# Two modulation stages and two norm stages at the head of a 1024-token kernel become one stage

## The chip, the cores and the metric

The kernel runs on one core of a Trainium2 chip. The metric is the device time of one execution in microseconds (us). A core has a matrix engine (TensorE, "PE" in the rows), a vector engine (VectorE, "DVE"), a scalar engine (ScalarE, "ACT"), GpSimd ("POOL") and SyncE ("SP"), which here issues nearly all of the DMA transfers. Each engine works through its own instructions in order; engines wait for one another by semaphores. SBUF is the on-chip memory with 128 partitions, PSUM the memory into which TensorE writes.

## The reference, cut to what matters

The model has two conditioned layers and then a second block of linear attention and experts. Only its head matters here. For each of the two layers a vector of 3 x 1024 modulation values is worked out for the latent tokens and another for the context tokens. The first layer's shift and scale are applied to the normed input:

```python
cond_l = jax.nn.silu(c)[:, None, :]
cond_c = jax.nn.silu(c_ctx)[None, None, :]
for layer in range(DEPTH):
    shift_l, scale_l, gate_l = jnp.split(cond_l @ w_ada[layer] + b_ada[layer], 3, axis=-1)
    shift_c, scale_c, gate_c = jnp.split(cond_c @ w_ada[layer] + b_ada[layer], 3, axis=-1)
    hl = rms_norm(x, norm_g[layer]) * (1.0 + scale_l) + shift_l
    hc = rms_norm(xc, norm_g[layer]) * (1.0 + scale_c) + shift_c
    ...
```

`w_ada` is (2, 1024, 3072) in float32, 12.6 MB for each layer; `x` has 1024 rows of 1024 features, `ctx` 256 rows. `hl` and `hc` are then multiplied by the layer's input weights `w_in0`.

## The kernel before

The program is a chain of stages. A `Stage` holds its SBUF and PSUM buffers and its semaphores, and inside it one block gives each engine its own instruction list; at a block's end all engines meet. So no instruction of a stage begins before the last of the stage before it has ended. The stages at the head, in order:

- `const` loads the identity matrix for transposes.
- `ada_0` and `ada_1` (`ada_stage`, lines 162 to 227) work out the modulation values of layer 0 and layer 1. The 3072 columns are cut into six chunks of 512. For each chunk, SP loads a weight piece `ada_w` of 2.1 MB (L190) and a bias piece (L192); TensorE multiplies with the two condition vectors as the stationary operand (L217), eight tiles of the inner dimension, each of which the trace shows as two records, so 16 a chunk; VectorE adds the bias (L227); SP stores two rows of 512 values to `ada` in DRAM (L196). There are two weight buffers, and the weights of chunk c + 2 are asked for when the matmuls of chunk c have ended.
- `n0l` (1024 latent rows) and `n0c` (256 context rows) are `norm_stage`, lines 230 to 378, two tiles of 128 rows a round. At its start SP loads gain, scale and shift, each spread over 128 partitions as 128 x 1024 (L269). For each tile: ScalarE squares and sums (L354), VectorE makes the mean (L316), GpSimd the power -0.5 (L366), VectorE multiplies by it and by the gain (L323) and adds the shift (L327), TensorE transposes in eight pieces of 128 x 128 (L378), and VectorE writes the result as a high part (L334) and a remainder (L337) into `h`, features by tokens.
- `in0` (`gemm_stage`) loads its first weight piece (L678), VectorE splits it in two (L718, L720), and TensorE begins (L706).

Semaphores are given out stage by stage and taken back by `recycle`, which clears them and lets all engines meet when more than a given number are out: 140 at the end of each stage. A later stage, `on0` (`out_norm`), already has the form of norm that the new stage uses: the rows are multiplied by the row's factor alone (L604), transposed (L483), and ScalarE applies scale and shift per feature as it takes them out of PSUM (L523), before VectorE splits them (L616, L618). It loads gain, scale and shift with features on partitions, as single elements of 4 bytes (L439).

Of the kernel before, what the change touches and what calls it, by code (L numbers as in the profile page):

```python
# [13 lines left out]
ACT = mybir.ActivationFunctionType  # L14
# [3 lines left out]
P = 128  # L18
D = 1024
KT = D // P  # L20
# [3 lines left out]
BANK = 512  # L24
EPS = 1e-6
# [4 lines left out]
F32R = mybir.dt.float32r  # L30
# [131 lines left out]
def ada_stage(nc, name, cond, w, b, out):  # L162

    N, cw = 3 * D, BANK
    rounds = N // (2 * cw)
    w_v = w.rearrange("(k p) n -> p k n", p=P)
    with Stage(nc, name) as st:
# [9 lines left out]
        with nc.Block() as block:  # L177

            @block.sync
            def _(sp):  # L180
                for j in range(2):
                    sp.dma_start(craw[:, j, :], cond[j].rearrange("(k p) -> p k", p=P), allow_slow_non_contiguous=True).then_inc(c_in, 16)
                for s in range(2):
                    w_in[s].open(sp)
                    o_out[s].open(sp)

                def load(it, s):
                    cols = ds((it * 2 + s) * cw, cw)
# [12 lines left out]

            @block.scalar
            def _(act):
                act.wait_ge(c_in, 32)
                for j in range(2):
                    act.activation(cond_t[:, :, j], craw[:, j, :], ACT.Silu).then_inc(c_ok, 1)

            @block.tensor
            def _(te):
                pe.open(te)  # L210
                te.wait_ge(c_ok, 2)
                with te.Fori(0, rounds) as it:
                    for s in range(2):
                        te.wait_ge(*w_in[s].now(it))
                        te.wait_ge(*dve.before(it, f"add{s}"))
                        for k in range(KT):
                            mm = te.matmul(ps[s][:], cond_t[:, k, :], wt[s][:, k, :], start=k == 0, stop=k == KT - 1)  # L217
                        mm.then_inc(*pe.did(f"mm{s}"))

            @block.vector  # L220
            def _(ve):
                dve.open(ve)
                with ve.Fori(0, rounds) as it:
                    for s in range(2):
                        ve.wait_ge(*pe.now(it, f"mm{s}"))
                        ve.wait_ge(*o_out[s].before(it))
                        ve.tensor_tensor(ot[s][:], ps[s][:], bt[s][:], ALU.add).then_inc(*dve.did(f"add{s}"))  # L227


def norm_stage(nc, name, ident, rows, x, norm_g, *, y=None, gate=None, scale=None, shift=None, x_out=None,  # L230
# [3684 lines left out]
def model(nc, x, c, ctx, c_ctx, norm_g, w_ada, b_ada, w_in0, sink0, gm_ln_g, gm_ln_b, gm_ws, gm_bs,  # L3915
# [10 lines left out]
    L = slice(0, S)  # L3926
# [5 lines left out]
    with ExitStack() as mem:  # L3932
        sb = lambda name, shape, dt=F32: mem.enter_context(nc.sbuf_tensor(name, shape, dt))
        ident_t, half_t = sb("ident", [P, P]), sb("half", [P, 1])
        with Stage(nc, "const") as st:
            loaded, ready = st.sem("loaded"), st.sem("ready")
            with nc.Block() as block:

                @block.sync
                def _(sp):  # L3940
                    sp.dma_start(ident_t[:], eye).then_inc(loaded, 16)
                    sp.wait_ge(loaded, 16)
# [19 lines left out]
        latent = ExitStack()  # L3962
# [124 lines left out]
```

## Time and profile before

| | us |
|---|---|
| median of 3 runs | 4587.3 |
| lowest and highest | 4581.42, 4588.21 |
| the profiled execution, its own time | 4582.68 |
| its span in the trace | 4580.8 |
| TensorE busy | 3749.5 |
| VectorE busy | 1923.9 |
| ScalarE busy | 1094.5 |
| GpSimd busy | 797.6 |

Busy shares are means over a program with many stages of different kinds. The mean granted TensorE clock of the span is 0.891 of full. In a row of a timeline the first number is the start in us from the span's start and the second the duration; "x32" joins 32 records in sequence; what stands in brackets is how long the engine had been idle and what ended that. "SPq" rows are DMA issues by SyncE: their duration is that of issuing, not of the transfer.

### The profile page before, as it was taken

Reading aid. Unit: us, or ns where it says so; the run is one execution under the profiler, and the core shown is the slowest. Engines: PE = TensorE matmul, PEld = TensorE weight load, DVE = VectorE, ACT = ScalarE, POOL = GpSimd, SP = SyncE. Lnnn points to the kernel's source line nnn. Section 1 sums busy time; section 2 is a strip of 40 time slices with the busy share of each in tenths; the row PEclk is TensorE's granted clock in tenths of the full one; section 3 lists DMA queues with packets and bytes.
Section 4 is the critical chain, followed back from the end, with each engine's and each line's share of the span. In section 5 each row is a group of like instructions: output and inputs, shape, how many; then the busy total and the mean of one; then the engine's idle time right before and its main releaser. Section 6 shows DMA issues by size and latency. Waiting matters only on the chain. (4 is left out here: it accounts for less than half of the span.)

```text
span 4580.8 us, 61052 instructions
## 1 busy us (share of the span) xinstructions
PE 3749.5 (82%) x24272; PEld 2811.9 (61%) x24272; DVE 1923.9 (42%) x2972; ACT 1094.5 (24%) x1970; POOL 797.6 (17%) x703
## 2 busy tenths in 40 slices
PE   7399799478859999977999899885879996759991
PEld 1299644467634444446988788662479995746661
DVE  0511144542137888855223255404546667211113
ACT  0111123222023444441111122215223333111111
POOL 0000000000013444440000021202134441020002
PEclk9699789588969999988999999886989997779996
DMA  6322200331110000002311144221333436379975
GB/s 221 111 85 72 72 7 12 123 108 50 50 37 3 4 3 3 3 28 103 114 60 64 62 101 102 93 71 35 87 105 95 120 97 236 138 261 335 326 242 197
DMA packets 333288, 462.23 MB, mean 101 GB/s; under 512 B 88853, under 2 KB 238821, under 8 KB 331765
## 3 DMA queue, kind: packets, MB, share of 16 engines
q1 hardware_dynamic: 325482, 433.18, 29.5%
q0 software_dynamic: 7568, 25.70, 1.5%
q8 instruction: 170, 2.79, 0.3%
q14 instruction: 68, 0.56, 0.0%
HBM read 350.73 MB, written 107.99 MB: 100 GB/s over the span
## 5 line engine op out<-in xcount | busy, mean ns | idle before, releaser
L2130 PE MATMUL gp_ps_p<-gp_wh,m 128*128 128x512 f32 (+1 forms) x1408 | 410.0, 373 | 7.5 <-DVE gp_wl L2174 7.5
L706 PE MATMUL in_ps_p<-in_wh,h 128*128 128x352 f32 x1280 | 309.5, 325 | 15.0 <-DVE in_wl L720 15.0
L2130 PEld LDWEIGHTS gp_ps_p<-gp_wh,m 128*128 128x128 f32 x1408 | 260.8, 189 | 47.7 <-DVE gp_wl L2174 8.0
L2130 PE MATMUL gp_ps_p<-gp_wl,m 128*128 128x512 f32 (+1 forms) x704 | 262.1, 372 | 0.0
L3785 PE MATMUL ex_ps_g<-ex_wgu,ex_xt 128*128 128x256 f32 x1024 | 234.8, 389 | 27.1 <-ACT ex_xt L3819 13.3
L1960 DVE TENSOR_REDUCE lq_nc<-lq_ps_f 128x1 f32<-128x512 f32 (+1 forms) x384 | 215.0, 585 | 59.3 <-PE lq_ps_f L1814 56.5
L1915 ACT ACTIVATE lq_p<-lq_ps_s 128x512 f32<-128x512 f32 x320 | 191.1, 598 | 181.5 <-PE lq_ps_s L1836 172.6
L706 PEld LDWEIGHTS in_ps_p<-in_wh,h 128*128 128x128 f32 x1280 | 224.1, 190 | 15.3 <-issue 15.3
L3785 PEld LDWEIGHTS ex_ps_g<-ex_wgu,ex_xt 128*128 128x128 f32 x1024 | 196.2, 194 | 60.7 <-DVE ex_xt L3836 19.4
L474 PE MATMUL on_ps_a<-on_wh,m 128*128 128x512 f32 x576 | 188.2, 404 | 43.1 <-DVE on_wl L567 36.5
L2034 POOL TENSOR_TENSOR lq_acc<-lq_acc,lq_p 128x512 f32<-128x512 f32 x128 | 172.1, 1345 | 242.2 <-ACT lq_p L1915 241.7
L706 PE MATMUL in_ps_p<-in_wl,h 128*128 128x352 f32 x640 | 207.0, 323 | 0.0
L2297 PE MATMUL cg_ps_p<-m,cg_wh 128*128 128x512 f32 x768 | 183.3, 397 | 0.0
L1982 DVE TENSOR_TENSOR lq_acc<-lq_acc,lq_p 128x512 f32<-128x512 f32 x128 | 167.8, 1311 | 15.6 <-ACT lq_p L1915 13.8
L1814 PE MATMUL lq_ps_f<-lq_kh,lq_qh 96*128 96x512 f32 (+1 forms) x384 | 143.9, 404 | 25.2 <-DVE lq_nc L1960 15.9
L2297 PEld LDWEIGHTS cg_ps_p<-m,cg_wh 128*128 128x128 f32 x768 | 144.7, 191 | 29.5
L3078 PE MATMUL dr_ps_big<-dr_px,dr_pn 64*64 64x128 f32 (+1 forms) x3072 | 160.5, 245 | 0.3 <-issue 0.3
L1846 PE MATMUL lq_ps_o<-lq_p,lq_v 128*64 128x512 f32 x640 | 159.4, 620 | 0.0
L474 PEld LDWEIGHTS on_ps_a<-on_wh,m 128*128 128x128 f32 x576 | 112.6, 196 | 68.8 <-DVE on_wl L567 37.8
L1836 PE MATMUL lq_ps_s<-lq_qh,lq_kh 97*128 97x512 f32 x320 | 147.5, 461 | 0.0
L2130 PEld LDWEIGHTS gp_ps_p<-gp_wl,m 128*128 128x128 f32 x704 | 132.8, 189 | 20.0
L3078 PEld LDWEIGHTS dr_ps_big<-dr_px,dr_pn 64*64 64x64 f32 x3072 | 137.6, 135 | 3.3 <-issue 3.1
(551 smaller groups left out, 7372.8 us busy)
## 6 DMA issues: line engine op xcount, KB each, us to landing
ex_wgu<-in_moe_w_gate_dram SPq DMA_DIRECT2D x32, 1024.0 KB, 8.2
ex_wgu<-in_moe_w_up_dram SPq DMA_DIRECT2D x32, 1024.0 KB, 10.7
ex_wd<-in_moe_w_down_dram SPq DMA_DIRECT2D x32, 1024.0 KB
ada_w<-in_w_ada_dram SPq DMA_DIRECT2D x12, 2048.0 KB
gp_w<-in_w_in_dram SPq DMA_DIRECT2D x32, 512.0 KB, 4.3
dr_qk<-feat SPq DMA_DIRECT2D x32, 512.0 KB, 4.2
yb<-ex_y SPq DMA_DIRECT2D x32, 512.0 KB
p<-in_o SPq DMA_DIRECT2D x8, 1760.0 KB, 7.2
```

Source lines behind the costliest of these rows:

```text
L474: mm = te.matmul(acc[i % NA][:, b, :], a, c, start=k == 0 and p == 0, stop=k == KT - 1 and p == 2)
L706: mm = te.matmul(ps[n % NB][:, 0:cw], a, b, start=n_ == 0, stop=n_ == len(todo) - 1)
L1836: mm = te.matmul(ps[e][t % 2][:], k_[e][b][:, cols], q_[e][c][:], start=n == 0, stop=n == 2)
L1846: mm = te.matmul(po[e * VC:(e + 1) * VC, :], vt[:, kt, h * VC:(h + 1) * VC], pt[e][t % NBUF][:], start=kt == 0, stop=kt == nk - 1)
L1915: act.activation(pt[e][t % NBUF][:], ps[e][t % 2][:], ACT.Exp, scale=scale).then_inc(exp_s, 1)
L1960: ve.tensor_reduce(nc_[v % 2][:, i, c:c + 1], f[:, 0:hi - lo], AX.X, ALU.max, negate=True).then_inc(freed_s[n % RING], 1)
L1982: ve.tensor_tensor(a[:], pt[0][(t - 1) % NBUF][:] if kt == 1 else a[:], pt[0][t % NBUF][:], ALU.add).then_inc(add_a, 1)
L2034: gp.tensor_tensor(a[:], pt[1][(t - 1) % NBUF][:] if kt == 1 else a[:], pt[1][t % NBUF][:], ALU.add).then_inc(add_b, 1)
L2130: mm = te.matmul(ps[i][:, 0:width[c]], a, b, start=k == 0 and p == 0, stop=k == KT - 1 and p == 2)
L2297: mm = te.matmul(ps[u % 2][:, hf, :], a[:, k, :], h_t[:, h, k, cols].bitcast(F32R), start=part == 0 and n == 0, stop=part == 1 and n == le ...
L3078: mm = te.matmul(b4[rows, h, js], P_[rows, h, :], old[rows, h, js, :], start=True, stop=True)
L3785: mm = te.matmul(pg[s % 2][:, g * DE:(g + 1) * DE], x_t[s][:, k * P:(k + 1) * P], wgu[s][:, g, k, :], start=k == 0, stop=k == KT - 1)
```

## The change

A new function `ada_norm` takes the place of `ada_0`, `ada_1`, `n0l` and `n0c`. It is one stage. The twelve weight chunks of both layers run in one sequence through three weight buffers. All ten tiles of rows stay in SBUF (`an_x`); their loads stand in SP's list after chunks 0 to 3, three, three, three and one. Their squares, sums and row factors are worked out while the chunks run. After chunk 3 the scale and shift of layer 0 are complete in DRAM; SP waits for these stores and loads them with features on partitions. The transposes stand in TensorE's list in pairs of tiles after chunks 5, 6, 7, 8 and 9. ScalarE applies scale and shift, VectorE splits into `h`. A second `recycle` with the bound 80 stands before `latent_pairs`.

```diff
+def ada_norm(nc, ident, half, cond, w_ada, b_ada, ada, segs, g, h_t):
...
+    cw, WB, X = BANK, 3, range(2)
+    per = 3 * D // cw
+    NC_ = 2 * per
+    need = 2 * D // cw
...
+    turns = {need + 1 + j: [2 * j, 2 * j + 1] for j in range(n // 2)}
...
+            @block.sync
+            def _(sp):
+                def weights(c):
+                    s, b = divmod(c, per)
+                    if c >= WB:
+                        sp.wait_ge(mm_s, c - WB + 1)
+                    sp.dma_start(wt[c % WB][:], w_ada[s].rearrange("(k p) n -> p k n", p=P)[:, :, b * cw:(b + 1) * cw]).then_inc(w_in[c % WB], 16)
+                    if c >= 2:
+                        sp.wait_ge(add_s, c - 1)
+                    sp.dma_start(bt[c % 2][:], b_ada[s].rearrange("(a n) -> a n", a=1)[:, b * cw:(b + 1) * cw].to_broadcast([2, cw])).then_inc(b_in[c % 2], 16)
...
+                for c in range(WB - 1):
+                    weights(c)
+                sp.dma_start(g_t[:], g.rearrange("(k p) -> p k", p=P), allow_slow_non_contiguous=True).then_inc(g_in, 16)
+                at = 0
+                for c in range(NC_):
+                    if c + WB - 1 < NC_:
+                        weights(c + WB - 1)
+                    for i in range(at, min(at + 3, n)):
+                        sp.dma_start(xt[i][:], src[i]).then_inc(x_in[i], 16)
+                    at = min(at + 3, n)
+                    store(c)
+                    if c == need - 1:
+                        for b in X:
+                            sp.wait_ge(o_out[b], 16 * (need // 2))
+                        for k in range(len(segs)):
+                            for t, part in ((sc_t, 1), (sh_t, 0)):
+                                sp.dma_start(t[:, k, :], ada[0][k, part * D:(part + 1) * D].rearrange("(k p) -> p k", p=P),
+                                             allow_slow_non_contiguous=True).then_inc(p_in, 16)
...
+            @block.tensor
+            def _(te):
+                te.wait_ge(c_ok, 2)
+                for c in range(NC_):
+                    te.wait_ge(w_in[c % WB], 16 * (c // WB + 1))
+                    if c >= 2:
+                        te.wait_ge(add_s, c - 1)
+                    for k in range(KT):
+                        mm = te.matmul(ps[c % 2][:], cond_t[:, k, :], wt[c % WB][:, k, :], start=k == 0, stop=k == KT - 1)
+                    mm.then_inc(mm_s, 1)
+                    for i in turns.get(c, []):
+                        te.wait_ge(hn_s, i + 1)
+                        if i >= 2:
+                            te.wait_ge(af_s, i - 1)
+                        for k in range(KT):
+                            tr = te.transpose(tp[i % 2][:, k // 4, (k % 4) * P:(k % 4 + 1) * P], xt[i][:, k * P:(k + 1) * P], ident)
+                        tr.then_inc(tr_s, 1)
...
+                for i in range(n):
+                    act.wait_ge(tr_s, i + 1)
+                    if i >= 2:
+                        act.wait_ge(e1_s, i - 1)
+                    for k in range(KT):
+                        ins = act.activation(tmp[i % 2][:, k, :], tp[i % 2][:, k // 4, (k % 4) * P:(k % 4 + 1) * P], ACT.Identity,
+                                             bias=sh_t[:, seg_of[i], k:k + 1], scale=sc_t[:, seg_of[i], k:k + 1])
+                    ins.then_inc(af_s, 1)
...
+                done = 0
+                for c in range(NC_):
+                    bias(c)
+                    if c < need:
+                        top = min(done + 3, n)
+                        for i in range(done, top):
+                            scaled(i)
+                        for i in range(done, top):
+                            normed(i)
+                        done = top
+                    if c == need:
+                        ve.wait_ge(g_in, 16)
+                        ve.wait_ge(p_in, 32 * len(segs))
+                        for k in range(len(segs)):
+                            ve.scalar_tensor_tensor(sc_t[:, k, :], sc_t[:, k, :], 1.0, g_t[:], ALU.add, ALU.mult).then_inc(gg_s, 1)
+                    for i in turns.get(c - 1, []):
+                        leave(i)
...
-        for i in range(2):
-            ada_stage(nc, f"ada_{i}", [c[0], c_ctx], w_ada[i], b_ada[i], ada[i])
...
-            for nm, rows, src, r in (("n0l", L, x, 0), ("n0c", X, ctx, 1)):
-                norm_stage(nc, nm, ident, rows.stop - rows.start, src, norm_g[0], scale=part(ada[0], r, 1), shift=part(ada[0], r, 0),
-                           h_t=h[:, :, :, rows])
+            ada_norm(nc, ident, half, [c[0], c_ctx], w_ada, b_ada, ada, [(len(lat), x), (len(con), ctx)], norm_g[0], h[:, :, :, :])
...
+            recycle(nc, 80)
```

In `ada_norm`, `bias(c)` waits for the matmuls of chunk c and adds the bias; `scaled(i)` waits for the square of tile i; `normed(i)` waits for GpSimd's power and multiplies the tile; `leave(i)` waits for ScalarE and splits tile i into `h`.

SyncE's list in the kernel before, from the third weight piece of `ada_0` on (a loop of three rounds): `ada_w` is a weight piece, `ada_b` a bias piece, `ada<-ada_o` a store.

```order
L190 DMA ada_w<-in_w_ada_dram 128x8x512
L192 DMA ada_b<-in_b_ada_dram 2x512
L196 ISA
L196 DMA ada<-ada_o 2x512
L189 REGISTER_ALU
L190 ISA
```

The same place in the changed kernel, from the fifth weight piece to the seventh: `an_w` is a weight piece, `an_b` a bias piece, `an_x` a tile of rows, `an_sc` and `an_sh` the scale and shift per feature.

```order
L266 DMA an_w<-in_w_ada_dram 128x8x512
L269 DMA an_b<-in_b_ada_dram 2x512
L286 DMA an_x<-in_x_dram 128x1024 x2
L286 DMA an_x<-in_ctx_dram 128x1024
L274 DMA ada<-an_o 2x512
L266 DMA an_w<-in_w_ada_dram 128x8x512
L269 DMA an_b<-in_b_ada_dram 2x512
L286 DMA an_x<-in_ctx_dram 128x1024
L274 DMA ada<-an_o 2x512
L294 DMA an_sc<-ada 128x8x1
L294 DMA an_sh<-ada 128x8x1
```

The row loads and the four element-wise loads now stand between weight pieces; the pair of scale and shift is issued twice, and the seventh weight piece (chunk 6) follows it.

VectorE's list in the changed kernel, from the bias of chunk 0 to that of chunk 2 (`an_o` is a chunk's result, `an_ss` the row factors):

```order
L350 TENSOR_TENSOR an_o0<-an_ps_p0,an_b0 2x512
L354 TENSOR_SCALAR an_ss<-an_ss 128x1 x3
L358 TENSOR_SCALAR an_x0<-an_x0,an_ss 128x1024
L358 TENSOR_SCALAR an_x1<-an_x1,an_ss 128x1024
L358 TENSOR_SCALAR an_x2<-an_x2,an_ss 128x1024
L350 TENSOR_TENSOR an_o1<-an_ps_p1,an_b1 2x512
```

Before, two bias additions followed each other with nothing between them; now three tiles' row factors and products stand between them.

TensorE's list in the changed kernel, from chunk 5 to chunk 7 (`an_ps_t` receives the transposes):

```order
L307 MATMUL an_ps_p1<-an_w2,an_cond 2x512 x8
L314 MATMUL an_ps_t0<-ident,an_x0 128x128 x8
L314 MATMUL an_ps_t1<-ident,an_x1 128x128 x8
L307 MATMUL an_ps_p0<-an_w0,an_cond 2x512 x8
L314 MATMUL an_ps_t0<-ident,an_x2 128x128 x8
L314 MATMUL an_ps_t1<-ident,an_x3 128x128 x8
L307 MATMUL an_ps_p1<-an_w1,an_cond 2x512 x8
```

The transposes, which had stages of their own behind the last chunk, stand between chunks of the same sequence.

## Rows read from the trace of the kernel before

**Rows 1.** The head of the page: span and instruction count.

```profile
span 4580.8 us, 61052 instructions
```

**Rows 2.** Timeline of the head of the program, 0 to 201 us.

```profile
4.24 0.37 SPq L190 DMA_DIRECT2D ada_w<-in_w_ada_dram  x1
...
12.12 15.73 PE L217 MATMUL ada_ps_p<-ada_w,ada_cond 128*2 128x512 f32 x32 [12.12 <-DMA ada_b<-in_b_ada_dram]
...
21.11 0.68 DVE L227 TENSOR_TENSOR ada_o<-ada_ps_p,ada_b 2x512 f32<-2x512 f32 x1 [21.11 <-PE ada_ps_p L217]
21.18 0.40 SPq L190 DMA_DIRECT2D ada_w<-in_w_ada_dram  x1
...
29.14 13.90 PE L217 MATMUL ada_ps_p<-ada_w,ada_cond 128*2 128x512 f32 x32 [1.29 <-DMA ada_b<-in_b_ada_dram]
...
102.56 14.18 PE L217 MATMUL ada_ps_p<-ada_w,ada_cond 128*2 128x512 f32 x32 [1.12 <-DMA ada_b<-in_b_ada_dram]
...
119.16 0.38 SPq L269 DMA_DIRECT2D n0l_g<-in_norm_g_dram  x1
...
200.28 11.68 SPq L678 DMA_DIRECT2D in_w<-in_w_in_dram  x3
```

**Rows 3.** Groups of instructions, 0 to 211 us; busy us, mean ns, idle.

```profile
L217 PE MATMUL ada_ps_p<-ada_w,ada_cond 128*2 128x512 f32 x192 | 87.4, 612 | 29.4 <-DMA ada_b<-in_b_ada_dram 29.1
...
L354 ACT ACTIVATE n0l_sq<-n0l_x 128x1024 f32<-128x1024 f32 x8 | 8.5, 1057 | 88.8 <-DMA n0l_x<-in_x_dram 87.2 <-DVE h L334 1.6
```

**Rows 4.** Windows while one weight piece moves; last: clock, DMA share, GB/s.

```profile
24.00:25.00 1.00, 1.00 (x3) 0.17 (x2) 0.00 (x0) 0.00 (x0) 0.00 (x0) 1.00 1.03 399
...
28.00:29.00 1.00, 0.00 (x0) 0.00 (x0) 0.56 (x1) 0.00 (x0) 0.00 (x0) 1.00 0.16 53
```

**Rows 5.** Timeline of stage `on0`, the new norm's operations.

```profile
1020.32 2.88 ACT L523 ACTIVATE on_tmp<-on_ps_t,on_sh,on_sc 128x128 f32<-128x128 f32 x8
...
1023.24 0.69 DVE L616 CAST m<-on_tmp 128x1024 fp32r<-128x1024 f32 x1 [4.00 <-ACT on_tmp L523]
...
1023.97 1.23 DVE L618 TENSOR_TENSOR m<-on_tmp,m 128x1024 fp32r<-128x1024 f32 x1
...
1025.33 0.55 POOL L546 TENSOR_TENSOR on_ss<-on_ss,half 128x1 f32<-128x1 f32 x1 [14.24 <-DVE on_ss L583]
...
1025.92 0.75 DVE L604 TENSOR_SCALAR on_h<-on_x,on_ss 128x1024 f32<-128x1024 f32 x1 [0.66 <-POOL on_ss L546]
...
1028.33 1.03 PE L483 MATMUL on_ps_t<-ident,on_h 128*128 128x128 f32 x8
```

**Rows 6.** Timeline of stage `on0`, five element-wise loads by SyncE.

```profile
967.10 0.44 SPq L439 DMA_DIRECT2D on_g<-in_norm_g_dram  x1
...
971.83 0.58 SPq L439 DMA_DIRECT2D on_sh<-ada  x1
...
974.27 0.24 DVE L623 SCALAR_TENSOR_TENSOR on_sc<-on_sc,on_g 128x8 f32<-128x8 f32 x2 [1.56 <-DMA on_sh<-ada]
```

**Rows 7.** Windows around idle TensorE; third from the end: granted clock.

```profile
121.00:122.00 1.00, 0.00 (x0) 0.00 (x0) 0.00 (x0) 0.00 (x0) 0.00 (x0) 0.83 1.11 168
...
122.00:123.00 1.00, 0.00 (x0) 0.00 (x0) 0.00 (x0) 0.00 (x0) 0.00 (x0) 0.50 0.72 262
...
70.00:73.00 3.00, 2.69 (x4) 0.47 (x5) 0.00 (x0) 0.00 (x0) 0.00 (x0) 0.50 1.04 388
...
74.00:75.00 1.00, 1.00 (x3) 0.17 (x2) 0.00 (x0) 0.00 (x0) 0.00 (x0) 1.00 0.70 256
```

**Rows 8.** Timeline at two stage ends, with and without `recycle`.

```profile
1251.36 0.60 ACT L1640 ACTIVATE gate_t<-in1g_ps_p 128x512 f32<-128x512 f32 x1 [4.84 <-PE in1g_ps_p L1633]
...
1253.82 0.37 SPq L678 DMA_DIRECT2D in1c_w<-in_w_in_dram  x1
...
1317.39 0.59 ACT L1540 ACTIVATE kpe_t<-lp_ps_t 32x512 f32<-32x512 f32 x1 [0.49 <-PE lp_ps_t L1586]
...
1318.31 0.38 SPq L1754 DMA_DIRECT2D lq_p<-in_w_kvb_dram  x1
```

More of the change, by code:

```diff
@@ L227, in _, with store, bias, scaled @@
                         ve.tensor_tensor(ot[s][:], ps[s][:], bt[s][:], ALU.add).then_inc(*dve.did(f"add{s}"))
+def ada_norm(nc, ident, half, cond, w_ada, b_ada, ada, segs, g, h_t):
[3 more added lines that the diff above has]
+    need = 2 * D // cw
+    n = sum(seg[0] for seg in segs)
+    seg_of = [k for k, seg in enumerate(segs) for _ in range(seg[0])]
+    src = [seg[1][i * P:(i + 1) * P, :] for seg in segs for i in range(seg[0])]
+    turns = {need + 1 + j: [2 * j, 2 * j + 1] for j in range(n // 2)}
+    order = [i for c in sorted(turns) for i in turns[c]]
+    assert order == list(range(n)) and max(turns) < NC_
+    with Stage(nc, "an") as st:
+        craw, cond_t = st.sb("craw", [P, 2, KT]), st.sb("cond", [P, KT, 2])
+        wt = [st.sb(f"w{b}", [P, KT, cw]) for b in range(WB)]
+        bt, ot = ([st.sb(f"{t}{b}", [2, cw]) for b in X] for t in ("b", "o"))
+        xt = [st.sb(f"x{i}", [P, D]) for i in range(n)]
+        sq, ss = st.sb("sq", [P, D]), st.sb("ss", [P, n])
+        g_t, sc_t, sh_t = st.sb("g", [P, KT]), st.sb("sc", [P, 2, KT]), st.sb("sh", [P, 2, KT])
+        tmp = [st.sb(f"t{b}", [P, KT, P]) for b in X]
+        ps = [st.ps(f"p{b}", [2, cw]) for b in X]
+        tp = [st.ps(f"t{b}", [P, 2, BANK]) for b in X]
+        c_in, c_ok, g_in, p_in, gg_s = (st.sem(t) for t in ("c_in", "c_ok", "g_in", "p_in", "gain"))
+        w_in, b_in, o_out = ([st.sem(f"{t}{b}") for b in range(k)] for t, k in (("w_in", WB), ("b_in", 2), ("o_out", 2)))
+        x_in = [st.sem(f"x_in{i}") for i in range(n)]
+        mm_s, add_s, sq_s, va_s, rs_s, hn_s, tr_s, af_s, e0_s, e1_s = (st.sem(t) for t in (
+            "mm", "add", "square", "var", "rsqrt", "hn", "tr", "affine", "ev0", "ev1"))
+        with nc.Block() as block:
+            @block.sync
[8 more added lines that the diff above has]
+                    sp.dma_start(bt[c % 2][:], b_ada[s].rearrange("(a n) -> a n", a=1)[:, b * cw:(b + 1) * cw].to_broadcast([2, cw])).then_inc(b_in[c % 2], 16)
+                def store(c):
+                    s, b = divmod(c, per)
+                    sp.wait_ge(add_s, c + 1)
+                    sp.dma_start(ada[s][:, b * cw:(b + 1) * cw], ot[c % 2][:]).then_inc(o_out[c % 2], 16)
+                for j in X:
+                    sp.dma_start(craw[:, j, :], cond[j].rearrange("(k p) -> p k", p=P), allow_slow_non_contiguous=True).then_inc(c_in, 16)
+                for c in range(WB - 1):
[16 more added lines that the diff above has]
+                                             allow_slow_non_contiguous=True).then_inc(p_in, 16)
+                for b in X:
+                    sp.wait_ge(o_out[b], 16 * (NC_ // 2))
+            @block.tensor
[15 more added lines that the diff above has]
+                        tr.then_inc(tr_s, 1)
+            @block.scalar
+            def _(act):
+                act.wait_ge(c_in, 32)
+                for j in X:
+                    act.activation(cond_t[:, :, j], craw[:, j, :], ACT.Silu).then_inc(c_ok, 1)
+                for i in range(n):
+                    act.wait_ge(x_in[i], 16)
+                    if i:
+                        act.wait_ge(sq_s, i)
+                    act.activation(sq[:], xt[i][:], ACT.Square, accum_out=ss[:, i:i + 1]).then_inc(sq_s, 1)
+                act.wait_ge(gg_s, len(segs))
+                for i in range(n):
+                    act.wait_ge(tr_s, i + 1)
[5 more added lines that the diff above has]
+                    ins.then_inc(af_s, 1)
+            @block.gpsimd
+            def _(gp):
+                for i in range(n):
+                    gp.wait_ge(va_s, i + 1)
+                    gp.tensor_tensor(ss[:, i:i + 1], ss[:, i:i + 1], half, ALU.pow).then_inc(rs_s, 1)
+            @block.vector
+            def _(ve):
+                def bias(c):
+                    ve.wait_ge(mm_s, c + 1)
+                    ve.wait_ge(b_in[c % 2], 16 * (c // 2 + 1))
+                    if c >= 2:
+                        ve.wait_ge(o_out[c % 2], 16 * (c // 2))
+                    ve.tensor_tensor(ot[c % 2][:], ps[c % 2][:], bt[c % 2][:], ALU.add).then_inc(add_s, 1)
+                def scaled(i):
+                    ve.wait_ge(sq_s, i + 1)
+                    ve.tensor_scalar(ss[:, i:i + 1], ss[:, i:i + 1], 1.0 / D, EPS, ALU.mult, ALU.add).then_inc(va_s, 1)
+                def normed(i):
+                    ve.wait_ge(rs_s, i + 1)
+                    ve.tensor_scalar(xt[i][:], xt[i][:], ss[:, i:i + 1], None, ALU.mult).then_inc(hn_s, 1)
+                def leave(i):
+                    rows = slice(i * P, (i + 1) * P)
+                    ve.wait_ge(af_s, i + 1)
+                    ve.tensor_copy(h_t[:, 0, :, rows].bitcast(F32R), tmp[i % 2][:]).then_inc(e0_s, 1)
+                    ve.wait_ge(e0_s, i + 1)
+                    ve.tensor_tensor(h_t[:, 1, :, rows].bitcast(F32R), tmp[i % 2][:], h_t[:, 0, :, rows], ALU.subtract).then_inc(e1_s, 1)
+                done = 0
[15 more added lines that the diff above has]
+                        leave(i)
+                for i in turns.get(NC_ - 1, []):
+                    leave(i)
```

## The prediction

> **What bounds the kernel now.** I read the head of the page for the span [rows 1], then the timeline of the head of the program [rows 2], since the change touches nothing else but one `recycle`. Stages do not overlap, so what the head takes adds to the end in full: `in0` cannot ask for its first weight piece before 200.28 us. The whole question is by how much that issue moves.
>
> In [rows 2] the reader is to see three stretches. (a) `ada_0` asks for its first weights at 4.24 and TensorE starts at 12.12; the twelve chunks of both stages end at 102.56 + 14.18 = 116.74. Twelve at 6.9 (below) would be 83 of these 105 us; the rest is the second start, waits of 1.1 to 1.3 us before each pair, and the low clock after each start. (b) The norm stage's first issue stands at 119.16, 2.4 us after that last matmul: bias, store, landing, meeting. (c) From 119.16 to 200.28, 81.1 us, the two norm stages run. They hold ten tiles on a chain of VectorE, and TensorE hardly works.
>
> The grouped rows [rows 3] give the floor: 192 matmul records busy for 87.4 us in the ada stages, and only 29.4 us of idle before them. A pair of chunks takes 13.90 us without a disturbance [rows 2], so 6.9 us each; the first pair, which starts at the low speed, takes 15.73. VectorE's first bias stands at 21.11, so chunk 0 ends at about 21.1.
>
> **What the change does, step by step.** The unit is the time at which TensorE ends chunk c, E(c); E(0) = 21.1 stays, as the first issues are the same.
>
> Transfers. A weight piece asked for at 21.18 on an empty queue serves TensorE at 29.14 at the latest [rows 2]. While it moves the queue carries 399 GB/s, and by 28 to 29 us it is empty [rows 4]; I take 390 GB/s. So 2.1 MB take 5.4 us, with 1.5 us before and 1.0 behind. A tile of rows (0.52 MB) takes 1.35. I assume that the queue serves in the order of issue.
>
> Chunks 0 to 3 hold the row work. Bias 0 ends at 21.8. SP then issues a bias piece and three tiles (2.0 us until the first moves), the tiles move for 4.0, and the last lands 1.0 later. ScalarE's square is 1.06 [rows 3], with its accumulator read about 1.25. VectorE's mean and GpSimd's power take 0.2 and 0.55, three products 0.75 each [rows 5], the next bias 0.68 [rows 2]. The sum is 11.5 with the gaps between them, so biases 1, 2 and 3 end at 33.3, 44.8 and 56.3, where TensorE's own pace would be 6.9. What is queued behind: VectorE can't add bias c + 1 while it waits for the rows of round c, and SP holds back the next bias piece, and with it the rows and the next weights, until that bias is added. The third buffer carries chunks 1 to 3 (E(1) = 27.9, E(2) = 34.8, E(3) = 41.7). Weights 4, behind three tiles, land at 45.8: TensorE waits 4.1. Weights 5 land at 57.3 where E(4) = 52.7: it waits 4.6. E(5) = 64.2.
>
> Parameters. After bias 3 (56.3) the tenth tile and the store move, behind weights 5; the store has landed at about 61. Then SP issues the four element-wise loads. Their price is shown by the same form in `on0`: five such loads take from 967.10 to 974.27, 7.2 us, of which SP issues until 972.4 [rows 6]. I take 1.3 us of SP for each, 5.2 together (bounds: 0.6 each, as the last one's 0.58, and 2.0). VectorE has its parameters near 68.6 and delays only bias 5. But weights 6 are asked for behind these loads, at 66.3, and land at 66.3 + 1.5 + 5.4 + 1.0 = 74.2. TensorE ends chunk 5 and its pair of transposes at 64.2 + 2.1 = 66.3 (1.03 us for eight [rows 5]) and waits 7.9. That is the dearest wait of the new stage.
>
> From chunk 6 on the transfers are ahead (weights 7 and 8 land near 79.6 and 85.0), and TensorE sets the pace: 6.9 + 2.1 = 9.0 us for chunks 6 to 9, 6.9 for 10 and 11. Beside it, a pair of tiles costs ScalarE 2 x 2.88 and VectorE 2 x (0.69 + 1.23) [rows 5]. Their chain over the two buffers is bias 0.7, one split 2.0, two outputs 5.8: 8.5 us a round. It hides under 9.0, but by half a microsecond only. So E(11) = 74.2 + 4 x 9.0 + 2 x 6.9 = 124.0.
>
> Clock. Idle TensorE loses its full clock some 5 us after its last matmul: it ended at 116.74 and the granted clock is 0.83 in the row of 121 to 122 and 0.50 in the next. After the restart at 70.3 it stays at 0.50 (1.2 GHz) until about 74, then 1.00 (2.4 GHz) [rows 7]. The waits of 4.1 and 4.6 are at the edge; what they would cost is hidden by the next wait for weights. The wait of 7.9 is past it and nothing hides the restart: 15.73 - 13.90 = 1.8 us [rows 2]. E(11) = 125.8.
>
> End. From the last matmul to the next stage's first issue 2.4 us, as now. `in0` asks for its weights at 128.2 instead of 200.28: 72 us less. What `in0` does from there is the same.
>
> `recycle`. With 10 semaphores fewer at the head, the clearing moves from behind `in1g` to behind `latent_prep`, and the new call with 80 finds none out. With it a stage end takes 1.9 us (ACT ends 1251.96, issue 1253.82), without it 0.3 (1317.98, 1318.31) [rows 8]: one is saved, one is paid, nothing is left.
>
> Removed without a separate term: gain, scale and shift spread over 128 partitions (six loads of 512 KB), VectorE's product with the gain and its addition of the shift, both inside the 81.1 us.
>
> **The rivals.**
> 1. Transfers hide everything: three buffers and early rows are enough. Then E(11) = 21.1 + 11 x 6.9 + 5 x 2.1 = 107.5 and the gain is 90 us: 4497. For it speaks that all bytes (30 MB at 390 GB/s, 78 us) fit under the matmuls. Against it, the chain of 11.5 us a round, which bandwidth doesn't shorten.
> 2. ScalarE and VectorE are the bound behind chunk 5, or SP's four loads take 2.0 each. The half microsecond of cover goes if an output takes a tenth longer: +4 to +8 us over four rounds; dearer loads add 3. Gain 60 to 68: 4519 to 4528.
> 3. The clock doesn't come back after the wait of 7.9. Six chunks at 13.7 and four pairs at 3.6 make E(11) = 171; the gain is 27: 4560. Were the whole stage at the low clock, 12.1 + 12 x 13.7 + 5 x 3.6 = 194.5 gives 197 against 200.28, no change that can be told. Against it: in both ada stages the clock is full within 4 us [rows 7], with TensorE as busy as here. The Trainium skill has the rule that speaks for this rival (TensorE: Matmul & The Clock Gate, section HAM oscillation): a kernel that waits for a transfer at each tile sees its clock fall at each of them, and with the three waits here in a row it would give the 4560 of this paragraph at worst.
> 4. Slower than before: the element-wise loads. They are 4096 pieces of 4 bytes on SP's only queue, and weights 6 stand behind them. They would have to take 72 us more than I count, 77 instead of 5. [rows 6] shows 5120 such pieces within 7.2 us; that would need over ten times the price, perhaps because they now share the queue with weights.
>
> The Trainium skill (DMA: Bandwidth & Descriptors, Specifications) states that line rate needs 512 B or more and that smaller pieces are read, changed and written back. The rule speaks for rival 4's direction; the trace has the price at the size in question.
>
> **How the numbers follow.** The schedule above: 0.60, gain 64 to 80. Rival 2: 0.15. Rival 1, whole or in good part: 0.15. Rival 3, whole or in part: 0.08, of which 0.02 without any measurable change. Rival 4: 0.02. The sum is made against the profiled execution, 4582.7 with its span of 4580.8 [rows 1]: 4510.7. The median of the runs shown is 4.6 us higher, so I predict 4587.3 - 72 = 4515. The range 4499 to 4531 takes in rival 2, the likeliest case and the partial form of rival 1. About 0.2%, 9 us, is what a measurement of this kernel can tell from no change. Faster by more: 0.96; within: 0.02; slower: 0.02.
>
> **What would show it.** In the trace after: `in_w` issued near 128 us; bias additions of the new stage some 11 us apart at chunks 1 to 3; three waits of TensorE for weights before chunks 4, 5 and 6, the last the longest; after it, starts of chunks 9 us apart and a granted clock of 1.00; no wait of TensorE for ScalarE. The prediction is wrong if rows land much earlier or later than 7 us after their issue begins, if weights overtake rows in the queue, or if VectorE's work on ten tiles reaches behind chunk 11.

## The result

The changed kernel takes 4501.6 us (median of four runs, 4489.9 to 4508.3) against 4587.3 of the kernel before (four runs, 4581.4 to 4588.2): ratio 0.9821, 95% interval 0.9806 to 0.9836. It is faster by 86 us; 72 had been forecast, with a range of 4499 to 4531. Three later comparisons stand under the experiments; two with this same kernel give 0.9802 (0.9780 to 0.9823) and 0.9804 (0.9785 to 0.9824), so the first one is the smallest of three.

The profiled execution is the fastest of its four, 4489.9 us. The head of its page has the span and TensorE's busy time, to be held against [rows 1]:

```profile
span 4488.1 us, 60788 instructions
...
PE 3727.8 (83%) x24272; PEld 2796.0 (62%) x24272; DVE 1900.9 (42%) x2962; ACT 1123.4 (25%) x2048; POOL 796.8 (18%) x701
```

The timeline of the head of the program answers to [rows 2]. `an_ps_p` rows of TensorE are weight chunks (x16 is one chunk), `an_ps_t` rows transposes:

```profile
12.45 29.11 PE L307 MATMUL an_ps_p<-an_w,an_cond 128*2 128x512 f32 x64 [12.45 <-DMA an_w<-in_w_ada_dram]
...
21.00 0.68 DVE L350 TENSOR_TENSOR an_o<-an_ps_p,an_b 2x512 f32<-2x512 f32 x1 [21.00 <-PE an_ps_p L307]
...
25.63 1.06 ACT L326 ACTIVATE an_sq<-an_x 128x1024 f32<-128x1024 f32 x1 [19.14 <-DMA an_x<-in_x_dram]
...
31.76 0.67 DVE L350 TENSOR_TENSOR an_o<-an_ps_p,an_b 2x512 f32<-2x512 f32 x1
...
42.38 0.67 DVE L350 TENSOR_TENSOR an_o<-an_ps_p,an_b 2x512 f32<-2x512 f32 x1
...
44.44 7.03 PE L307 MATMUL an_ps_p<-an_w,an_cond 128*2 128x512 f32 x16 [2.88 <-DMA an_w<-in_w_ada_dram]
...
53.26 0.67 DVE L350 TENSOR_TENSOR an_o<-an_ps_p,an_b 2x512 f32<-2x512 f32 x1
...
54.64 0.29 SPq L274 DMA_DIRECT2D ada<-an_o  x1
...
55.26 8.72 PE L307 MATMUL an_ps_p<-an_w,an_cond 128*2 128x512 f32 x16 [3.79 <-DMA an_w<-in_w_ada_dram]
...
57.72 0.38 SPq L294 DMA_DIRECT2D an_sc<-ada  x1
...
60.27 0.58 SPq L266 DMA_DIRECT2D an_w<-in_w_ada_dram  x1
...
68.34 7.03 PE L307 MATMUL an_ps_p<-an_w,an_cond 128*2 128x512 f32 x16 [2.46 <-DMA an_w<-in_w_ada_dram]
...
77.20 7.03 PE L307 MATMUL an_ps_p<-an_w,an_cond 128*2 128x512 f32 x16
```

The same timeline from chunk 8 to `in0`:

```profile
86.05 7.03 PE L307 MATMUL an_ps_p<-an_w,an_cond 128*2 128x512 f32 x16
...
103.77 13.89 PE L307 MATMUL an_ps_p<-an_w,an_cond 128*2 128x512 f32 x32
...
117.70 0.68 DVE L350 TENSOR_TENSOR an_o<-an_ps_p,an_b 2x512 f32<-2x512 f32 x1 [2.46 <-PE an_ps_p L307]
...
120.31 1.02 SPq L836 DMA_DIRECT2D in_w<-in_w_in_dram  x2
```

The reader is to see three things. First, chunks 0 to 3 run in one piece (29.11 us for 64 records, no wait in it), then TensorE waits 2.88, 3.79 and 2.46 us for the weights of chunks 4, 5 and 6, and never again. Second, VectorE's biases of chunks 1, 2 and 3 stand at 31.76, 42.38 and 53.26, a good 10.6 us apart, although the matmuls of these chunks were done by then (those of chunk 3 ended at 41.56); in the trace before the first two such rows stood at 21.11 and 27.88, 6.8 us apart. Third, from chunk 6 on a chunk begins every 8.86 us (77.20, 86.05). `in0` asks for its weights at 120.31 instead of 200.28: 80.0 us earlier, 7.9 more than forecast.

The groups for the same stretch, against [rows 3]: the matmuls cost what they cost before (86.9 us), their idle time is down from 29.4 to 21.6 us, of which 12.4 is the start, and the transposes are 9.8 us with no idle ahead of them.

```profile
L307 PE MATMUL an_ps_p<-an_w,an_cond 128*2 128x512 f32 x192 | 86.9, 610 | 21.6 <-DMA an_w<-in_w_ada_dram 21.6
...
L333 ACT ACTIVATE an_t<-an_ps_t,an_sh,an_sc 128x128 f32<-128x128 f32 x80 | 28.5, 496 | 22.6 <-DVE h L365 16.7 <-PE an_ps_t L314 5.9
...
L314 PE MATMUL an_ps_t<-ident,an_x 128*128 128x128 f32 x80 | 9.8, 276 | 0.0
```

The span is 92.7 us shorter, though, and 80.0 of that lie ahead of `in0`. The other 12.7 lie behind it, in stages whose instructions the change leaves as they are. The first experiments are about that.

### The profile page after: what moved, and what is told of

Read it like the earlier page. It is cut to its first block and busy times, and to the rows that moved or that the text cites. A ratio compares the mean times of both kernels' runs of the same rounds, so it can differ in the third digit from the quotient of the medians.

```text
span 4488.1 us, 60788 instructions
## 1 busy us (share of the span) xinstructions
PE 3727.8 (83%) x24272; PEld 2796.0 (62%) x24272; DVE 1900.9 (42%) x2962; ACT 1123.4 (25%) x2048; POOL 796.8 (18%) x701
## 6 DMA issues: line engine op xcount, KB each, us to landing
ex_wgu<-in_moe_w_up_dram SPq DMA_DIRECT2D x32, 1024.0 KB, 10.7
```

## The experiments

"The issue" is the start of `in0`'s first weight load in a run's own trace. It measures the new stage alone; whole times scatter by some 10 us each way.

**1. The changed kernel again, unaltered, and a third time.**

> The changed kernel once more, unaltered. In the first trace in0 asked for its weights at 120.31 us, 80.0 earlier than before, yet the span was 92.7 shorter. Theory A (the change acts at the head alone; the other 12.7 us are scatter between executions, four runs lay between 4490 and 4508): the issue stands again at 120.3 within half a us, and the time from there to the end of the span, 4367.8 in the first trace, comes out longer, nearer to the 4380.5 of before. Theory B (the stages behind became shorter through the moved clearing of semaphores or other addresses): the rest is again 4368 within 3 us.

> The changed kernel a third time. In two traces in0 asked at 120.3 and 125.0 us; the difference lay in the waits for weights 4 to 6 and in slow matmuls behind them. Theory (which of the waits is long enough to lose the clock is a matter of a few tenths of a us and of the execution): again between 119 and 126, with one or two chunks of more than 8 us among chunks 4 to 6. Rival (the second run's chip was slower): 120.3 again, one such chunk.

The issue stood at 124.95 in the second trace and at 122.54 in the third; the rest was 4375.9 and 4365.8. TensorE's chunks 4, 5 and 6 in the second trace:

```profile
45.85 8.33 PE L307 MATMUL an_ps_p<-an_w,an_cond 128*2 128x512 f32 x16 [3.14 <-DMA an_w<-in_w_ada_dram]
...
56.69 7.03 PE L307 MATMUL an_ps_p<-an_w,an_cond 128*2 128x512 f32 x16 [2.51 <-DMA an_w<-in_w_ada_dram]
...
70.20 9.81 PE L307 MATMUL an_ps_p<-an_w,an_cond 128*2 128x512 f32 x16 [4.58 <-DMA an_w<-in_w_ada_dram]
```

and in the third:

```profile
45.05 8.72 PE L307 MATMUL an_ps_p<-an_w,an_cond 128*2 128x512 f32 x16 [3.54 <-DMA an_w<-in_w_ada_dram]
...
55.77 8.72 PE L307 MATMUL an_ps_p<-an_w,an_cond 128*2 128x512 f32 x16 [2.00 <-DMA an_w<-in_w_ada_dram]
...
68.88 8.72 PE L307 MATMUL an_ps_p<-an_w,an_cond 128*2 128x512 f32 x16 [2.49 <-DMA an_w<-in_w_ada_dram]
```

A chunk takes 7.03 us at full clock and 8.3 to 9.8 where it restarts at the low one. The first trace has one such chunk, the second two, the third three, of one and the same program, behind waits of much the same length. With the length of the waits it makes the scatter of the head, 120.3 to 125.0 us. My expectation that the head repeats within half a us was wrong, and the rest of the second trace, 4375.9, fits neither of its two theories. For the third run the issue lay between 119 and 126 as expected, but with three slow chunks and not one or two. Whole times: 4495.8 (five runs) against 4584.6, and 4491.4 (four) against 4585.7.

**2. The chunks merged, the norm stages left.** `ada_norm` without its rows, then the old loop, and the second `recycle` as in the changed kernel:

```diff
-            ada_norm(nc, ident, half, [c[0], c_ctx], w_ada, b_ada, ada, ...)
+        ada_only(nc, [c[0], c_ctx], w_ada, b_ada, ada)   # sync, tensor and vector lists of ada_norm, without rows
...
+            for nm, rows, src, r in (("n0l", L, x, 0), ("n0c", X, ctx, 1)):
+                norm_stage(nc, nm, ident, ...)
```

> The twelve chunks in one stage with three weight buffers, but without rows; the two norm stages as before. Theory: this removes the second start of the chunks (12.0 us of idle TensorE), one slow restart (1.8) and four waits of 1.1 to 1.3 before pairs (5.1), 18.9 in all: in0 asks at 181.4 instead of 200.3. Rival (two buffers were not the cause of the waits before pairs): they stay, 14 us, in0 asks at 186.

The time was 4560.1, ratio 0.9948 (0.9931 to 0.9966). TensorE ran all 192 records without a wait:

```profile
12.36 85.19 PE L280 MATMUL an_ps_p<-an_w,an_cond 128*2 128x512 f32 x192 [12.36 <-DMA an_w<-in_w_ada_dram]
```

```profile
181.43 11.84 SPq L747 DMA_DIRECT2D in_w<-in_w_in_dram  x3
```

The issue stood at 181.4, what the theory said; that it fits to the tenth is luck, since the head scatters by more. With three buffers and no rows in the queue the chunks have no wait at all, so the waits in the new stage come with the rows and parameters.

**3. The new stage with all transposes behind chunk 11.**

```diff
-    turns = {need + 1 + j: [2 * j, 2 * j + 1] for j in range(n // 2)}
+    turns = {NC_ - 1: list(range(n))}
```

> The new stage, but all ten tiles are transposed behind chunk 11 and none between chunks. Theory: chunks end at 109 to 110 us, then ScalarE sets the pace with 2.9 us a tile: 29 us, one split 2, in0 asks at 142, 22 us behind the changed kernel. Rival (ScalarE and VectorE hand each tile over and don't overlap, 4.9 us a tile): in0 asks at 160.

4520.7 us, ratio 0.9860 (0.9845 to 0.9875), issue at 145.2. Behind the last chunk ScalarE works in one piece and the others follow it, a tile each 2.8 us:

```profile
114.64 28.02 ACT L333 ACTIVATE an_t<-an_ps_t,an_sh,an_sc 128x128 f32<-128x128 f32 x80 [54.95 <-PE an_ps_t L314]
...
117.69 1.73 PE L314 MATMUL an_ps_t<-ident,an_x 128*128 128x128 f32 x8 [2.27 <-ACT an_t L333]
...
145.19 1.02 SPq L836 DMA_DIRECT2D in_w<-in_w_in_dram  x2
```

The tail is as the theory had it (31.7 us from the last matmul at 113.5); the chunks ended 4 us later than I had put them. From 2 and 3 the head's gain falls into three parts, by single traces: merging the chunks 18.9 us, the new form of the norm with rows loaded and scaled under the chunks 36.2, transposes and output between the chunks 24.9. Some 3.5 us of the last part are not the transposes' doing: chunk 6 began at 70.81 here instead of 68.34, and chunks 6 to 11 took 42.71 us where three pairs at full clock take 41.7.

Experiments 4 to 7 are one execution each. Their whole times, 4486.2, 4495.8, 4494.5 and 4497.9 us against 4587.7 of the kernel before, lie within those of the changed kernel (4482.4 to 4508.3) and rank nothing. Nor can two issues be told apart that differ by less than the 4.6 us between its three traces; what is read here are the waits inside one trace.

**4. Weights of chunk 6 ahead of the parameters.**

```diff
                     if c == need - 1:
+                        weights(need + WB - 1, "weights")
                         for b in X:
                             sp.wait_ge(o_out[b], 16 * (need // 2))
```

> Only the weights of chunk 6 are moved ahead of the wait for the stores and of the four element-wise loads. Theory (the wait of 2.5 us before chunk 6 comes from the parameters standing ahead of these weights): the wait is gone, in0 asks at 117.8 in place of 120.3, and the parameters arrive some 4 us later without anyone waiting long. Rival (the parameters then come too late for ScalarE, and the transposes of the second pair wait): the issue stays at 120 or later.

SyncE's issues, weights 6 first, then the first and the last parameter load; and TensorE's chunk 6 and the second tile of the pair behind it:

```profile
56.81 0.38 SPq L267 DMA_DIRECT2D an_w<-in_w_ada_dram  x1
...
59.71 0.38 SPq L298 DMA_DIRECT2D an_sc<-ada  x1
...
66.45 0.58 SPq L298 DMA_DIRECT2D an_sh<-ada  x1
```

```profile
66.72 7.03 PE L311 MATMUL an_ps_p<-an_w,an_cond 128*2 128x512 f32 x16 [0.71 <-DMA an_w<-in_w_ada_dram]
...
75.65 1.06 PE L318 MATMUL an_ps_t<-ident,an_x 128*128 128x128 f32 x8 [0.88 <-ACT an_t L337]
```

The wait before chunk 6 fell to 0.71 us, where the three plain traces have 2.46 to 4.58, so it had come from the order of the queue. The price of the rival appears too: the loads behind 2.1 MB took SyncE from 59.71 to 67.03 instead of 2.55 us, and a transpose waited 0.88 us for ScalarE. The issue stood at 119.75, with one slow chunk (8.50), and not at 117.8.

**5. Bias ahead of the rows.** VectorE's list: `if c < need:` becomes `if c and done < n:`, so that the rows of a round are worked on behind the next bias.

> VectorE adds bias c + 1 before it works on the rows of round c; three tiles a round as in the changed kernel. Theory 'chain' (my prediction's: SP gets the next round late because the bias is held back by the rows): both waits before chunks 4 and 5 (2.9 and 3.8) go, and with them the slow clock of chunk 5 (1.7): in0 asks at 112. Rival 'bandwidth' (a round moves 3.67 MB, 9.4 us at 390 GB/s, against 6.9 of TensorE): waits of some 2 and 2.6 stay, the issue moves by 3 us at most, to 117.

```profile
44.38 7.03 PE L307 MATMUL an_ps_p<-an_w,an_cond 128*2 128x512 f32 x16 [1.60 <-DMA an_w<-in_w_ada_dram]
...
53.64 7.03 PE L307 MATMUL an_ps_p<-an_w,an_cond 128*2 128x512 f32 x16 [2.23 <-DMA an_w<-in_w_ada_dram]
...
66.09 8.38 PE L307 MATMUL an_ps_p<-an_w,an_cond 128*2 128x512 f32 x16 [3.53 <-DMA an_w<-in_w_ada_dram]
```

The waits before chunks 4 and 5 are 1.60 and 2.23 us, 3.83 together; the plain traces have 5.5 to 6.7. They did not go: the rival was right about them, and removing the chain took away some three to four tenths. The queue shows why. The same microsecond in the changed kernel and here (the last number is GB/s):

```profile
33.00:34.00 1.00, 1.00 (x3) 0.17 (x2) 0.00 (x0) 0.00 (x0) 0.00 (x0) 1.00 0.33 80
```

```profile
33.00:34.00 1.00, 1.00 (x3) 0.17 (x2) 0.17 (x1) 0.00 (x0) 0.00 (x0) 1.00 1.07 397
```

In the changed kernel the queue runs low once a round, because SP is held back by the bias: there the chain does set the pace. With the bias out of the way the queue moves 383 to 414 GB/s in every microsecond from 26 to 53, and the bytes set it. The issue stood at 119.4; 117 had been the rival's.

**6. Two tiles a round for five rounds** (`done + 3` and `at + 3` to `+ 2`, without the bound on c).

> Two tiles of rows a round for five rounds in place of 3, 3, 3, 1; nothing else. Theory 'chain': a round is 10.7 less one tile's transfer and product, some 8.6 us, still above 6.9, so the waits before chunks 4 and 5 shrink to about 0 and 1, and one before chunk 6 grows since the fourth store is behind two tiles: in0 asks at 117 to 119. Rival 'no change': if the number of tiles matters only in sum, it stays at 120.3.

Waits of 0.73, 2.07 and 4.33 us for weights, then 0.60 and 1.74 for ScalarE, which now had the last squares ahead of the first output; issue at 121.4; 117 to 119 had been expected. The first wait shrank as expected, the later ones took it back.

**7. Parameters loaded twice.**

```diff
-                            for t, part in ((sc_t, 1), (sh_t, 0)):
+                            for t, part in ((sc_t, 1), (sh_t, 0), (sc2, 1), (sh2, 0)):
```

> The four element-wise loads of scale and shift are done twice (the second time into tiles that nobody reads). Theory (on a queue that has run dry such a load costs SP 0.6 us, 2.55 for four, as in the trace of the changed kernel): the wait before chunk 6 grows by 2.6 or somewhat more, in0 asks at 123 to 124. Rival (the price that I predicted, 1.3 us each): it grows by 5.2, in0 asks at 125.5. Should the loads cost nothing beyond their place behind the store, the issue stays at 120.3.

VectorE waits for all eight (its bound 32 becomes 64). SyncE, first parameter load to weights 6, and TensorE:

```profile
58.06 0.38 SPq L295 DMA_DIRECT2D an_sc<-ada  x1
...
63.69 0.58 SPq L267 DMA_DIRECT2D an_w<-in_w_ada_dram  x1
```

```profile
55.91 7.03 PE L308 MATMUL an_ps_p<-an_w,an_cond 128*2 128x512 f32 x16 [3.74 <-DMA an_w<-in_w_ada_dram]
...
72.19 9.84 PE L308 MATMUL an_ps_p<-an_w,an_cond 128*2 128x512 f32 x16 [7.35 <-DMA an_w<-in_w_ada_dram]
```

Eight loads hold weights 6 back by 5.63 us where four took 2.55: 3.1 for four more, 0.8 each. The wait before chunk 6 grew from 2.46 to 7.35, and the issue came at 127.0. These two sums look like the rival's (5.2 more, 125.5). But of the 4.9 us by which the wait grew, 3.4 are weights 6 asked for later, and 1.0 is that chunk 5 ran at full clock and TensorE was ready earlier (64.84 against 65.88). The length of the loads is read directly, and it is the theory's.

**8. All three edits, two tiles a round; and the same with the transposes one chunk later** (`need + 2 + j`).

> Two tiles of rows a round in place of three, VectorE adds bias c + 1 before it works on the rows of round c, and the weights of chunk 6 are asked for before the parameters. Theory 'bandwidth and order of the queue make the waits': 2.1 + 1.05 MB a round are 8.1 us, which the lead of the third buffer covers over five rounds; no wait of TensorE above 0.5 us, in0 asks at 109 to 110 us, 11 us before the changed kernel, total some 11 us less. Rival 'waits come from something else' (a slot, the clock): waits of 2 us or more stay and the issue stands behind 115.

4490.1 us, ratio 0.9796 (0.9783 to 0.9810), issue at 116.05, where 109 to 110 had been expected. For weights TensorE waited only 0.66. But ScalarE's list holds the tenth tile's square ahead of the first output, and two transposes waited for it:

```profile
62.35 1.06 ACT L330 ACTIVATE an_sq<-an_x 128x1024 f32<-128x1024 f32 x1 [9.72 <-DMA an_x<-in_ctx_dram]
...
64.79 9.54 ACT L337 ACTIVATE an_t<-an_ps_t,an_sh,an_sc 128x128 f32<-128x128 f32 x27
...
67.82 1.06 PE L318 MATMUL an_ps_t<-ident,an_x 128*128 128x128 f32 x8 [2.89 <-ACT an_t L337]
...
70.62 1.94 PE L318 MATMUL an_ps_t<-ident,an_x 128*128 128x128 f32 x8 [1.74 <-ACT an_t L337]
```

> The variant with all three edits, and the pairs of transposes one chunk later, behind chunks 6 to 10. In that variant TensorE waited 2.9 and 1.7 us for ScalarE, whose list holds the square of the tenth tile ahead of the first output. Theory: one chunk later that square is done, both waits go, the last split costs 2 us more at the end: in0 asks at 112, 4 us before that variant and 8 before the changed kernel. Rival (the waits come from the hand-over between ScalarE and VectorE over two buffers): they stay, in0 asks at 118.

4492.1 us, ratio 0.9803 (0.9789 to 0.9817), issue at 119.9. The waits for ScalarE went, and two for weights came in their place; I had expected no wait and 112:

```profile
58.88 7.03 PE L311 MATMUL an_ps_p<-an_w,an_cond 128*2 128x512 f32 x16 [2.17 <-DMA an_w<-in_w_ada_dram]
...
70.78 8.72 PE L311 MATMUL an_ps_p<-an_w,an_cond 128*2 128x512 f32 x16 [2.97 <-DMA an_w<-in_w_ada_dram]
```

The variant of 116.05 has the earliest issue seen, but its whole time differs from that of the changed kernel (0.9802 in the same comparison) by less than the intervals. No version was shown to beat the changed kernel.

**9. The kernel before again, and with the clearing of semaphores moved.**

```diff
-        recycle(self.nc, 140)
+        recycle(self.nc, 150)
```

> The kernel before once more, unaltered, for a second trace. Behind the head (from in0's first issue to the end) its first trace has 4380.5 us; seven traces of the changed kernel and its variants (all but the merge alone and the changed one's second) have 4365 to 4377. Theory A (scatter between executions alone): the second trace of before lies among those, 4365 to 4377. Theory B (something behind the head is shorter by some 9 us with the change): it lies at 4380 or above. The issue itself stands at 200.3 again in both.

> The kernel before, with the bound at a stage's end raised from 140 to 150 semaphores, so that they are cleared behind latent_prep instead of behind in1g (and, late in the program, one call later at the same place), as in the changed kernel. Theory (moving the clearing costs nothing and brings nothing): ratio 1.000 within 0.002; in1g's stage is 1.4 us shorter, latent_prep's 1.4 us longer. Rival (the moved clearing or other semaphore numbers make the rest of the program shorter): 8 to 10 us less than before, with its head unchanged at 200.3.

The kernel before against itself: 0.9998 (0.9988 to 1.0008), issue at 202.8, rest 4383.3, which is theory B. With the clearing moved: 4579.0, ratio 0.9989 (0.9978 to 0.9999), issue at 200.8, rest 4384.4. `in1g`'s stage is 1.4 us shorter in the trace, as in the changed kernel. Whether the moved clearing brings a few us is not decided: the medians differ by 6.7 us, the interval allows 0.5 to 10, and the trace, no shorter, is of an execution of 4587.0 us, 8 above the median of its kind. The second and third column and the last one below come from one chip, so the chip is not what makes the rest differ.

Durations between first issues, worked out from the timelines of six traces (us):

```
first issue to first  before  again  moved | changed  again  third
in0 to window         332.5  335.0  333.0 |  330.9   331.3  329.0
gdn_rounds            470.5  476.4  473.2 |  470.0   469.8  470.2
experts               437.0  437.0  436.6 |  435.8   435.7  434.7
latent_pairs on       852.7  849.1  853.3 |  850.2   851.9  848.3
all behind the issue 4380.5 4383.3 4384.4 | 4367.8  4375.9 4365.8
```

(The first line runs from `in0`'s first issue to that of the window stage's queries; the last but one from `latent_pairs` to the weight load of the stage behind it. Stages between these are left out.)

## Why the prediction was right, and where its sum was off

**The mechanism** held step by step: E(0), a round of rows longer than a chunk, three waits for weights before chunks 4, 5 and 6, then TensorE's own pace of 9 us (8.86 measured), no wait for ScalarE, 2.4 us from the last matmul to the next issue (2.6). One sign of it failed: the last of the three waits was to be the longest, 7.9 us. It was the longest only in the second trace (4.58); in the first it was the shortest (2.46). Rival 1, transfers that hide everything, did not come; rivals 2, 3 and 4 did not either. The issue at 120.3 to 125.0 lies 3 to 8 us ahead of the 128.2 forecast.

**How close it was.** Two errors went the same way: the head gained 80.0 us in the profiled execution and not 72, and some 12 us came behind the head, where none were forecast. The first median, 4501.6, is 2.6 us above the lower end of the range of 4499 to 4531. The two later ones of the same kernel, 4495.8 and 4491.4, lie below it. So the range held for the measurement it was made for, and in part by luck.

**The round of rows** was put at 11.5 us from bias to bias and measures 10.6 to 10.9: GpSimd's powers ran beside VectorE's products, which I had put one behind the other. (The terms that I listed make 11.9, not 11.5.) Three rounds make 2.4 us (53.93 against 56.3 for the end of bias 3). I had named VectorE's held-back bias as what bounds the round, and in the changed kernel it does: its queue runs low in each round. But I had counted the bytes over the whole stage only (78 us, rival 1) and not by the round, where 3.67 MB take 9.4 us at 390 GB/s, against 10.7 of the chain and 6.9 of TensorE. Experiment 5 shows this second bound: with the chain removed the waits before chunks 4 and 5 only shrank from 2.88 and 3.79 to 1.60 and 2.23. More than half of them would be there without the cause that I named.

**The parameters** were the single term that was mis-sized most. The store was put at 61.0 and the four loads at 5.2 us, weights 6 at 66.3. Measured: 57.72, 2.55 and 60.27. The price of 1.3 us each was taken from loads issued behind weights that were still moving; here the queue had run dry (1 to 8 GB/s), and experiment 7 gives 0.8 for each further one. Behind moving weights they take what `on0` showed, and more (experiment 4: 7.3 us for four). The wait for the store was put too long as well, by the 0.9 us below. The low bound of 0.6 that I had given was the right one.

**The ledger** of the 7.9 us by which `in0` came earlier than forecast in the profiled execution: shorter rounds 2.4; the store landed 0.9 sooner behind them; the loads 2.6. Weights 6 were asked for 6.0 us earlier (60.27 against 66.3), and their own way took 0.2 longer than put. The clock's 1.8 fell away, since chunk 6 ran at full clock there, and the four periods of 8.86 instead of 9.0 give 0.6. The stage end took 0.2 more, and the rest is rounding: 6.0 - 0.2 + 1.8 + 0.6 - 0.2 = 8.0 against 7.9.

The Trainium skill (DMA: Bandwidth & Descriptors, Specifications) has pieces under 512 B below line rate. By that rule the trace agrees: while the four loads ran, the queue moved 1 to 8 GB/s (the windows below, 58 to 61 us). It cost 2.6 us, not the 77 of rival 4.

**The clock** was put at 1.8 us behind the wait before chunk 6. Chunks 4 and 5 were put at nothing, since I read a loss "some 5 us" behind the last matmul from [rows 7], and since the next wait for weights would hide it. In the first trace the loss fell on chunk 5, behind a wait of 3.79. It cost nothing there, since TensorE had to wait for weights 6 all the same, and chunk 6 itself was fast. In the second and third traces chunk 6 did lose 2.8 and 1.7 us, in the place that was forecast, but behind waits of 4.58 and 2.49 and not of 7.9. The granted clock around chunk 5 in the first trace (0.50 is 1.2 GHz; columns as in [rows 7], the last is GB/s):

```profile
56.00:57.00 1.00, 1.00 (x3) 0.21 (x2) 0.00 (x0) 0.00 (x0) 0.00 (x0) 0.71 0.89 340
58.00:59.00 1.00, 1.00 (x2) 0.13 (x1) 0.00 (x0) 0.96 (x1) 0.00 (x0) 0.50 0.17 1
59.00:60.00 1.00, 1.00 (x3) 0.17 (x2) 0.15 (x1) 0.19 (x2) 0.54 (x1) 0.58 0.49 4
60.00:61.00 1.00, 1.00 (x4) 0.22 (x3) 0.96 (x2) 0.00 (x0) 0.01 (x1) 1.00 1.07 8
```

Behind the wait the granted clock fell to 0.50 within the row of 56 to 57 (0.71) and was back at 1.00 by 60 (0.58 in the row before); 8.72 us for the chunk instead of 7.03.

In the third trace waits of 3.54, 2.00 and 2.49 us all lost the clock; in experiment 7 one of 3.74 did not. The step "the loss begins past some 5 us" is wrong; how long TensorE waits does not alone decide it. The Trainium skill (TensorE: Matmul & The Clock Gate, section HAM oscillation) lets a kernel that waits for a transfer at each tile lose its clock at each. By that rule the third trace agrees, three waits and three slow chunks of 8.72 us, the first trace in one of three.

**`recycle`** came out as forecast: in the trace after, ACT ends `in1g` at 1166.12 and the next issue stands at 1166.62, 1.4 us less than before; at `latent_prep` it is 1230.05 and 1231.81, 1.4 us more.

**What the prediction left out.** Behind the head I had forecast no change. Three traces without the new stage have 4380.5 to 4384.4 us from the issue to the end; the three of the changed kernel 4365.8 to 4375.9, seven variants of it 4364.6 to 4376.7, and the merge alone (experiment 2) lies between them with 4377.9. So some 12 us, about a seventh of the whole gain, lie in stages with the same instructions in the same order, spread over several of them by 1 to 3 us each. Everything from the issue to the end, before and after (busy us and instructions of TensorE, its weight loads, VectorE, ScalarE, GpSimd; then granted clock, DMA share, GB/s):

```profile
200.28:4580.80 4380.52, 3644.08 (x24000) 2779.81 (x24000) 1864.48 (x2908) 1081.11 (x1945) 789.64 (x686) 0.89 0.30 98
```

```profile
120.31:4488.10 4367.79, 3631.72 (x24000) 2771.34 (x24000) 1866.05 (x2908) 1081.76 (x1945) 788.77 (x686) 0.90 0.31 98
```

The same 24000 matmul records were busy for 12.4 us less, and VectorE, ScalarE and GpSimd differ by less than 2 us. The other traces agree: 3643.2 and 3644.8 us without the new stage, 3640.4 and 3629.0 in the second and third of the changed kernel. So most of the 12 us are shorter matmuls, not waits that went. That fits a clock that was lost less often, but the means of 0.89 and 0.90 are too coarse to show it. What makes them shorter stays open; the moved clearing was tried (experiment 9) and is neither shown nor ruled out.

## What to carry to other kernels

Merge stages that leave the matrix engine idle, but count bytes per round before counting instructions: rows fetched between weight pieces were free only as far as weights and rows together fitted the time of a chunk. The place of a small load in the issuing engine's list matters more than its own price, since the next large piece waits behind it. Take the price of such a load from a place where the queue is in the same state, and when an edit removes one wait, look in the other engines' lists for what is next: twice here it was a single instruction in ScalarE's list or the weights of the next chunk.

## What the runs showed of the hardware

The same program lost TensorE's clock behind one, two or three of its waits in three executions; waits of 2.00 us lost it and one of 3.74 did not, at 1.3 to 2.8 us for each loss. Element-wise loads of 1024 pieces took SyncE 0.6 to 0.8 us each on an empty queue (2.55 us for four, 5.63 for eight). Behind weights in flight four took 7.3 us (experiment 4), and a single one up to 4.2 (experiment 8).
